# Loading four of thirteen expert weight slots through GpSimd's software queue

## What is computed

```python
def grouped_moe(h, router_w, router_bias, w_gate, w_up, w_down):
    scores = sigmoid(h @ router_w)            # 16 experts in 4 groups
    ...                                       # best group, its best 2 experts, gates
    y = zeros_like(h)
    for e in range(N_EXPERTS):                # 16, D_EXPERT = 512
        a = silu(h @ w_gate[e]) * (h @ w_up[e])
        y = y + dense_gates[:, e:e + 1] * (a @ w_down[e])
    return y

# per layer of the second block
h = layer_norm(ALPHA * h + mix, ln1_g[l], ln1_b[l])
h = layer_norm(ALPHA * h + grouped_moe(h, ...), ln2_g[l], ln2_b[l])
```

## Time and profile before

| | |
|---|---|
| median of three runs | 1690.81 us (1688.6 to 1694.21) |
| the profiled execution, its own time | 1684.51 us |
| its span, first to last instruction | 1682.7 us |
| mean granted TensorE clock | 0.966 |
| busy PE / DVE / ACT / POOL | 1567.5 / 930.2 / 624.3 / 49.8 us |
| DMA | 427.66 MB, mean 254 GB/s |
| of it SP's hardware queue | 417.43 MB, packets 67.8% of 16 engines |
| of it GpSimd's software queue | 8.87 MB, 1.8% |
| expert stages | about 1035 to 1264 us and 1442 to 1670 us of the span |

### The profile page before, as it was taken

One profiled execution on the slowest core, in us unless ns is written; L12 is line 12 of the kernel. 1 busy time (PEld: TensorE's weight loads), 2 busy tenths in 40 slices (PEclk: granted clock), 3 DMA queues, 4 the chain that ended last, 5 costly groups with the idle time before them and its releaser, 6 DMA issues.

```text
span 1682.7 us, 19021 instructions
## 1 busy us (share of the span) xinstructions
PE 1567.5 (93%) x7519; PEld 1072.6 (64%) x7519; DVE 930.2 (55%) x1401; ACT 624.3 (37%) x904; POOL 49.8 (3%) x66
## 2 busy tenths in 40 slices
PE   2899998999899998999989998999988999999996
PEld 2777787888778787788878774333336876433332
DVE  5888687865578978755467864111006786211002
ACT  2354544434344464444335742111114573111111
POOL 2000000000000000000030200000000110000000
PEclk8899999999999999999989998999998998999998
DMA  9677555976567734765565337999995417799995
GB/s 340 220 249 245 185 177 179 318 259 225 190 232 256 271 126 152 274 209 176 190 162 188 101 128 302 410 409 409 409 371 176 153 51 267 305 409 408 409 409 215
DMA packets 149980, 427.66 MB, mean 254 GB/s; under 512 B 8120, under 2 KB 16560, under 8 KB 149888
## 3 DMA queue, kind: packets, MB, share of 16 engines
q1 hardware_dynamic: 146208, 417.43, 67.8%
q0 software_dynamic: 3456, 8.87, 1.8%
q10 hardware_dynamic: 224, 0.07, 0.0%
HBM read 425.30 MB, written 1.05 MB: 253 GB/s over the span
## 4 chain that ended last, share of the span: by engine, by line
PE 62%; DVE 17%; DMA 7%; SPq 7%; ACT 4%; issue 3%; DVEq 0%; ACTq 0%
PE gp L2341 26%; PE gp L2788 9%; PE gp L2564 9%; SPq L756 6%; PE gp L2807 4%; DVE wlo L1424 4%; DMA raw<-in_w_in 3%; PE mp L2828 2%; DMA raw_deep<-in_exp_w_up 2%; PE gp L2773 2%; ACT whi L872 2%; DMA raw_deep<-in_w_ada 2%; DVE acc L1296 1%; DVE ft L1485 1%; PE mp L2625 1%
## 5 line engine op out<-in xcount | busy, mean ns | idle before, releaser
L1424 DVE TENSOR_TENSOR wlo<-raw,whi 128x2048 fp32r<-128x2048 f32 (+1 forms) x131 | 287.2, 2193 | 171.0 <-ACT whi L872 168.8
L872 ACT ACTIVATE whi<-raw 128x2048 fp32r<-128x2048 f32 (+1 forms) x131 | 240.0, 1835 | 297.3 <-PE gp L2341 162.7
L2341 PE MATMUL gp<-whi,xt_hi 128*128 128x512 f32 (+1 forms) x792 | 313.9, 396 | 16.7 <-DVE xt_lo L1495 7.4
L2341 PE MATMUL gp<-whi,xt_lo 128*128 128x512 f32 (+1 forms) x792 | 305.0, 385 | 0.0
L2341 PE MATMUL gp<-wlo,xt_hi 128*128 128x512 f32 (+1 forms) x792 | 304.7, 385 | 0.0
L2341 PEld LDWEIGHTS gp<-whi,xt_hi 128*128 128x128 f32 x792 | 151.0, 191 | 54.7 <-issue 14.4
L2341 PEld LDWEIGHTS gp<-whi,xt_lo 128*128 128x128 f32 x792 | 150.7, 190 | 30.2
L2341 PEld LDWEIGHTS gp<-wlo,xt_hi 128*128 128x128 f32 x792 | 151.0, 191 | 27.6 <-issue 1.0
L2196 DVE TENSOR_SCALAR pr<-slots,key,dg 128x128 f32<-128x128 f32 x64 | 19.3, 343 | 255.2 <-PE gp L2818 255.2
L1296 DVE SCALAR_TENSOR_TENSOR acc<-raw,cact,acc 128x1024 f32<-128x1024 f32 x69 | 88.5, 1282 | 2.6 <-DMA raw<-in_w_ada 1.1
L2210 DVE TENSOR_TENSOR pr<-pr,gp 64x512 f32<-64x512 f32 x32 | 21.7, 679 | 123.3 <-ACT pr L1214 123.3
(11 more groups left out here) (443 smaller groups left out, 2476.1 us busy)
## 6 DMA issues: line engine op xcount, KB each, us to landing
raw<-in_w_in SPq DMA_DIRECT2D x60, 1024.0 KB, 5.8
raw<-in_w_ada SPq DMA_DIRECT2D x42, 1024.0 KB, 5.3
raw_deep<-in_exp_w_gate SPq DMA_DIRECT2D x28, 1024.0 KB, 16.2
raw_deep<-in_exp_w_up SPq DMA_DIRECT2D x28, 1024.0 KB, 14.9
raw_deep<-in_exp_w_down SPq DMA_DIRECT2D x28, 1024.0 KB, 15.0
raw<-in_w_gate SPq DMA_DIRECT2D x20, 1024.0 KB, 5.1
raw<-in_w_up SPq DMA_DIRECT2D x20, 1024.0 KB, 5.2
raw<-in_w_down SPq DMA_DIRECT2D x20, 1024.0 KB, 5.0
```

The lines of the kernel that those rows point to most:

```text
L872: act.activation(halves1(s, l, units, cols)[0], slot(raw, g % RAW, units, cols), ACT.Copy).then_inc(hi_done.sem, 1)
L1424: dve.tensor_tensor(lo, slot(raw, g % RAW, units, cols), hi.bitcast(F32), ALU.subtract).then_inc(raw_read[g % RAW].sem, 1)
L2341: mm = pe.matmul(gp[:, q % 2, t, 0:wide], a[:, chunk, ts], w[:, unit, c0:c0 + wide], start=first and n == 0 and m == 0, stop=last and n == ...
```

## The change

Slots 3, 4, 5 and 12 (`raw_more` and `raw_extra`) are loaded by GpSimd, the nine others by SyncE as before. The order of units, the slots and all that TensorE does stay. SP no longer waits for `oa_ready`; GpSimd does, once a layer, ahead of its first expert load. GpSimd then goes through the units in the same order, loads those of its slots after waiting for `read`, and puts the wait for `h_ready`, the increment of `rows_free` and the two norm row loads ahead of unit 13, so behind its loads of units 3, 4, 5 and 12.

```diff
+        def issued_by_pool(n):
+            m = (n - S2_MOE) % DEEP
+            return m == EXTRA or RAW <= m < 2 * RAW
+
+        def expert_units(l):
+            for e in range(NE + 1):
+                if e < NE:
+                    for i in range(4):
+                        yield unit_at(e, i), expert_weights(l, e, i)
+                if e:
+                    for i in range(4, 6):
+                        yield unit_at(e - 1, i), expert_weights(l, e - 1, i)
...
                 def load(n, src):
                     part, there, read, before = ring2(n)
                     units, cols = src.shape[1:]
-                    if n == S2_MOE + RAW:
-                        sp.wait_ge(*oa_ready.at2(l, 1))
                     if n == S2_MOE + 2 * RAW:
                         sp.wait_ge(*w_used.at2(l, S2_MOE))
                     sp.wait_ge(*read.at2(l, before))
                     sp.dma_start(parts_of(part, units, cols), src).then_inc(there.sem, 16)
...
-                for e in range(NE + 1):
-                    if e < NE:
-                        for i in range(4):
-                            load(unit_at(e, i), expert_weights(l, e, i))
-                    if e:
-                        for i in range(4, 6):
-                            load(unit_at(e - 1, i), expert_weights(l, e - 1, i))
+                for n, src in expert_units(l):
+                    if not issued_by_pool(n):
+                        load(n, src)
...
-                pool.wait_ge(*h_ready.at2(l, 2))
-                pool.sem_inc(rows_free, 1)
-                norm_rows(A["ln2_g_2"][l], A["ln2_b_2"][l])
+                pool.wait_ge(*oa_ready.at2(l, 1))
+                for n, src in expert_units(l):
+                    if n == S2_MOE + DEEP:
+                        pool.wait_ge(*h_ready.at2(l, 2))
+                        pool.sem_inc(rows_free, 1)
+                        norm_rows(A["ln2_g_2"][l], A["ln2_b_2"][l])
+                    if issued_by_pool(n):
+                        part, there, read, before = ring2(n)
+                        units, cols = src.shape[1:]
+                        pool.wait_ge(*read.at2(l, before))
+                        pool.dma_start(parts_of(part, units, cols), src).then_inc(there.sem, 16)
```

## The result

The changed kernel takes 1718.08 us in the median of four runs (1714.95 to 1720.71), the kernel before 1691.78 us in four (1688.6 to 1694.21). The medians lie 26.3 us apart. The forecast was slower by 18.8 us, 1709, with a range up to 1717. The direction and the main mechanism held; the size did not, and one term that was put at nothing was not nothing.

A forecast was written before the change was run, and what follows sets the result against it. Transfers at 409 GB/s were taken to bound the expert stages. Landing order 7.7 plus clock 1.7 made 9.4 us a layer, 18.8 for two, on 1684.5, plus 6.3 to the median: 1709; range up to 1717, below to rates ending at 1693.

The forecast's parts named there:

- What bounds the kernel: Expert stages: transfers run full at 409 GB/s, PE is faster; its waits cost 5.07 us a layer.
- Order of landing: Expert stage's end: unit 89 lands later because GpSimd's units run ahead; main term, +7.7 us a layer.
- equal halves: Expert stage: both queues share the rate equally; a GpSimd unit takes about 5 us once its slot is free.
- The row that I took: Norm row loads: two 512 KB loads landed 2.47 us apart, 212 GB/s, read as half of 409.
- Issue cost: Expert stage: 30 units a layer move to GpSimd's issue; worth 0, since the other queue has work meanwhile.
- The clock: Last expert's first pair: a 3.4 us wait before it brings slow matmuls, +1.7 us a layer; bounds 0 and 3.65.
- The row I took: Expert stage before the change: after a 2.01 us wait, sixteen matmuls took 5.35 us instead of 3.65.
- Rate of the mixture: Expert stages with both queues busy: 409 GB/s taken; 403 would add 3.2 us, 426 would save 8.5.
- two queues carry no more than one: Answers the rival that two queues carry more: 1690 at 426 GB/s, floor 1680.7; 12 in 100.
- the landing order matters: Answers the rival that landing order doesn't matter, as GpSimd's units do not get ahead: 1691; 7 in 100.
- the software queue alone is not the slow one: Answers the rival that the software queue is slow: at 118 GB/s, 54 us more a layer, about 1799; 5 in 100.

The follow-up runs named there:

- one queue swapped: Kernel before, SyncE the only issuer, with units 90, 94 and 95 loaded ahead of 88 and 89 in each layer: ratio to before 1.0120.
- three units moved: Kernel before, with units 90, 94 and 95 of each layer issued by GpSimd: ratio to before 1.0126.
- the tail back on SyncE: Changed kernel, with units 83, 90, 94 and 95 returned to SyncE, so all loads from unit 83 on share one queue: ratio to before 1.0051.
- the kept-busy kernel: Changed kernel, with 16 extra identity transposes right ahead of the last expert's first pair: ratio to before 1.0157.
- the two experiments: Kernel before with its last loads reordered in SyncE's queue, and kernel before with units 90, 94, 95 on GpSimd: ratios 1.0120 and 1.0126.
- the extra transposes behind: Changed kernel, with 8 or 24 extra identity transposes behind the last expert's first pair of each layer: 1718.93 and 1715.59 us.

## Why the prediction missed

*What bounds the kernel* held. PE's periods, the idle gap ahead of the restart, 409 GB/s and the thirteen slots' lead are as read; the restart stands 3.7 us behind the start of the first pair in both (1035.57 to 1039.25 before, 1041.30 to 1044.98 after). One wait was overlooked, 0.42 us before expert 13's first pair (at 1209.36 before); it changes nothing in the sum.

*Order of landing*, the main term, held to a tenth: 7.7 us forecast, 7.8 measured in the changed kernel's second layer, 7.7 with one queue swapped, 7.6 to 7.9 with three units moved. In the first layer it is 9.9, for the reason below. The picture of equal halves held at the end. In the middle, waits of 2 us were forecast before the first pairs of experts 11 and 13; there were 3.0 (on the unit just ahead of that pair, in the first layer) and 3.3, and then 2.9 in both layers.

GpSimd's units were indeed the early ones, but I expected them 5 to 7 us after issue and they took mostly 10 to 15. Half of the rate is not the whole of it. The issue of one unit of the changed kernel that had GpSimd's queue to itself, the packets that moved in the next 3.9 us (1072.6 to 1076.5), and the packets from 1057.92 to 1061.7, where the unit just issued was SyncE's:

```profile
1072.60 0.71 POOL L850 DMA_DIRECT2D raw_extra<-in_exp_w_up  x1 [16.93 <-PE gp L2802]
```

```profile
q1 hardware_dynamic: 411, 1.59, 101.8%
```

```profile
q0 software_dynamic: 330, 1.29, 96.5%
```

In neither stretch did the queue with the new unit move a packet. Its first one came 3.9 us after issue at 1072.60, 3.8 us after issue at 1057.92, and 3.5 to 4.0 us wherever in an expert stage a queue was empty and the other was busy; with both queues empty it was 1.0 us for SyncE and 1.4 for GpSimd. The unit issued at 1072.60 landed at 1082.40, 9.8 us after issue: 3.9 before its first packet, and 5.9 of transfer, somewhat more than the 5.1 of half the rate. Units that stand behind one another in GpSimd's queue land mostly 5.1 us apart (1182.89, 1188.00, 1193.13). The row that I took had this in it: at half of 409 GB/s 512 KB are 2.6 us, and the norm row took 7.6. For the time it meant little here, because GpSimd's units had slack: unit 95 landed at 1253.87, 1.7 us ahead of unit 89, where I had all three by 1245.

*Issue cost*, "Worth 0, because the other queue has work while one issue is under way", failed at the restart of the first layer, where the other queue has none. SyncE's slots 0 to 2 and slot 3 are refilled; the next to come free are slots 4 and 5, both GpSimd's. The timelines of GpSimd, then of SyncE, in the changed kernel:

```profile
1048.72 0.71 POOL L850 DMA_DIRECT2D raw_more<-in_exp_w_gate  x1 [28.04 <-PE gp L2802]
1054.24 0.72 POOL L850 DMA_DIRECT2D raw_more<-in_exp_w_up  x1 [4.81 <-PE gp L2802]
1054.96 0.71 POOL L850 DMA_DIRECT2D raw_more<-in_exp_w_gate  x1
```

```profile
1045.39 3.39 SPq L766 DMA_DIRECT2D raw<-in_exp_w_down  x2
1057.92 0.37 SPq L766 DMA_DIRECT2D raw_deep<-in_exp_w_up  x1
```

PE freed slots 4 and 5 at 1053.55 (the pair at 1049.90 and 3.65 us); GpSimd's issue began 0.7 us later and took 0.72, where SyncE before issued within 0.1 us and took 0.37. SyncE's last unit landed at 1056.78, and its next one, issued at 1057.92, moved no packet before 1061.71, so GpSimd's queue stood alone. The transfers ran short, a stretch of the changed kernel:

```profile
1056.00:1060.00 4.00, 4.00 (x20) 1.58 (x18) 1.28 (x2) 0.59 (x1) 0.00 (x0) 1.00 0.90 308
```

308 GB/s for 4 us is 1.0 us lost; in all, the stream is 2.1 us longer (216.5 against 214.4), and what the stream loses the last pair waits for. The other 1.1 us is not placed: the trace shows only that the rate falls off before the end (264 GB/s from 1259 to 1261, 66 to 1263). In the second layer GpSimd's issue came 0.4 us sooner after the stage's start (12.55 us instead of 12.94) and the stream was not longer (214.4). The second profile of the changed kernel, the tail back on SyncE and the kept-busy kernel have the same two times and the same longer stream in the first layer alone. That the 0.4 us decide fits all of these, but no run changes them by themselves.

*The clock* was mis-sized in one layer: 1.7 us forecast, 1.5 and 2.6 measured, 2.5 in the two experiments. The row I took followed a 2.01 us wait; before the last pair, waits of 3.7 to 8.0 us are followed by 5.1 to 5.3 us in the changed kernel's first layer (also with the extra transposes behind) and by 6.1 to 6.3 everywhere else. That the first layer came near 1.7 is in part luck: the row says nothing of longer waits.

*Rate of the mixture* held: 409.

Together, the stages cost 11.4 + 10.4 = 21.8 us for the 18.8 forecast: 2.1 from the restart, about 0.7 from the clock, 0.2 from the main term. So the step that failed inside the sum is *Issue cost*, put at 0 on the ground that the other queue has work: at the first layer's restart it had none, and the last pair waited 2.1 us longer. That alone would have stayed inside the range. The remainder has no term in my sum at all: 5.5 us between the stages in the profiles, most of it dips of the granted clock in the second layer's attention part. 21.8 + 5.5 = 27.3, of the 28.6 by the ratio. This last sum is weaker than it looks: it takes two profiles of before, of 1684.51 and 1687.80 us, which had no dips in the second layer, and no execution of before at 1688.6 to 1694.21 us was profiled, so how often before has them is not known. What is sure is the 21.8. The range should have held such a part; the dips of the earlier trace rows and the 6.3 us by which the profiled execution lay below the median were signs that this kernel's time moves by several us without a cause in its work.

The rivals fell: two queues carry no more than one (409 GB/s in both kernels); the landing order matters (10.3 us a stage with one queue); the software queue alone is not the slow one (408 GB/s).

## What to carry over

Where one in-order queue feeds an engine that uses its data in order and the transfers are the limit, the order of the queue is hard to beat: none of the six other orders and splits tried here did. The second issuer added no bandwidth (409 GB/s either way), its queue took half of the rate whatever stood in the other, and that delayed the very unit that was waited for next. To price such a change, count the bytes still to come behind the last unit on which the engine waits, before and after; waits earlier in the stage are paid back. If a second issuer is wanted all the same, let the last ring of loads stand in one queue (2.3 and 0.8 us a stage here instead of 11.4 and 10.4), and look at the places where one queue runs empty: there its next unit starts late.

## What was not expected of the hardware

The software queue alone holds 408 GB/s over 180 us, as SyncE's does (409). A unit issued into an empty queue while the other queue keeps the engines busy moves its first packet 3.5 to 4.0 us later, with idle engines 1.0 us (SyncE) or 1.4 us (GpSimd). GpSimd mostly starts an issue 0.3 us after the slot is freed (0.7 at the restart of the first layer), SyncE within 0.1 us. Before the last pair, waits of 3.7 to 8.0 us are followed by sixteen matmuls of 5.1 to 6.3 us instead of 3.65, one of 2.0 us by 5.35, and sixteen small matmuls ahead of the wait (1.95 us of it left) bring back 3.65. The same piece of the attention part, with no wait of note, takes 15.2 us at a granted clock of 1.00 in some executions and 16.7 to 20.7 us at 0.90 to 0.67 in others.
